# Second-order Hyena filters between the first order's spectral products, and their norms applied after the convolution

## The reference

```
h = sin(fr * (feats @ w1 + b1)); h = sin(fr * (h @ w2 + b2)); h = h @ w3 + b3
h = h.reshape(L, N_DIR, HYENA_ORDER, D_HYENA)            # 512, 2, 2, 512
h = h * exp(-t * abs(decay))
fwd, bwd = h[:, 0], h[:, 1]
k = concatenate([fwd, zero, flip(bwd[1:])])              # circular, length 2L
k = k * rsqrt(sum(k * k, axis=0) + FILTER_EPS)           # one norm per order and channel
k_f = rfft(k)
z = x1 * (irfft(rfft(v) * k_f[:, 0])[:L] + d[0] * v)
z = x2 * (irfft(rfft(z) * k_f[:, 1])[:L] + d[1] * z)
```

## Time and profile before

| | us |
|---|---|
| median of 3 runs (lowest, highest) | 3144.1 (3139.53, 3148.76) |
| time of the profiled execution | 3137.39 |
| its span, first to last instruction | 3135.5 |
| `hyena_spectra`, first product to the next block's first transpose | 951.24 to 1022.29 |
| `hyena_long_convs`, to its last gating | 1022.29 to 1099.6 |

### The profile page before, as it was taken

How to read it: one execution, slowest core, us unless ns; L and a number is a source line. 1 busy time by engine, 2 the same in 40 slices (tenths; PEclk the granted TensorE clock), 3 DMA queues, 4 the chain that set the end, 5 groups by cost and what they waited for, 6 DMA issues and landing times. The chain is left out here.

```text
span 3135.5 us, 40381 instructions
## 1 busy us (share of the span) xinstructions
PE 2786.7 (89%) x17361; PEld 2194.9 (70%) x17361; DVE 1584.6 (51%) x2124; ACT 872.0 (28%) x1114; POOL 388.4 (12%) x368
## 2 busy tenths in 40 slices
PE   7999998778788889999998969589999659899997
PEld 5888875677563777788886844468887445678886
DVE  5555455666665734455544226553354545363342
ACT  3221234111144123322223323332222423332221
POOL 1111000211002001111100001121020100120110
PEclk9999999899889899999998978889999779989998
DMA  5555530000040033455543200223343200223221
GB/s 154 163 165 170 158 105 21 13 3 3 2 129 0 1 108 101 114 167 162 163 158 111 81 19 0 81 68 109 105 149 101 54 30 2 94 72 104 94 94 54
DMA packets 267298, 272.77 MB, mean 87 GB/s; under 512 B 10559, under 2 KB 248102, under 8 KB 266927
## 3 DMA queue, kind: packets, MB, share of 16 engines
q1 hardware_dynamic: 251760, 208.32, 21.7%
q0 software_dynamic: 15360, 61.87, 6.0%
HBM read 268.07 MB, written 2.10 MB: 86 GB/s over the span
## 5 line engine op out<-in xcount | busy, mean ns | idle before, releaser
L863 DVE TENSOR_TENSOR mlp_wl<-mlp_raw,mlp_wh 128x2048 fp32r<-128x2048 f32 x74 | 189.9, 2566 | 277.8 <-ACT mlp_wh L755 277.8
L863 DVE TENSOR_TENSOR mix_wl<-mix_raw,mix_wh 128x2048 fp32r<-128x2048 f32 (+2 forms) x66 | 153.1, 2319 | 236.9 <-ACT mix_wh L755 236.8
L673 PE MATMUL mix_ps<-h_mix_hi,mix_wh 128*128 128x512 f32 x624 | 245.8, 394 | 10.1 <-ACT mix_wh L755 10.1
L675 PE MATMUL mix_ps<-h_mix_lo,mix_wh 128*128 128x512 f32 x624 | 244.3, 391 | 0.0
L755 ACT ACTIVATE mlp_wh<-mlp_raw 128x2048 fp32r<-128x2048 f32 x74 | 140.5, 1899 | 142.7 <-PE mlp_ps L679 88.8
L755 ACT ACTIVATE mix_wh<-mix_raw 128x2048 fp32r<-128x2048 f32 (+2 forms) x66 | 117.6, 1782 | 219.8 <-PE mix_ps L679 162.1
L673 PE MATMUL ffn_ps<-h_rw_hi,ffn_wh 128*128 128x512 f32 x448 | 175.3, 391 | 0.0
L675 PE MATMUL ffn_ps<-h_rw_lo,ffn_wh 128*128 128x512 f32 x448 | 174.3, 389 | 0.0
L679 PE MATMUL mix_ps<-h_mix_hi,mix_wl 128*128 128x512 f32 x624 | 154.2, 389 | 0.0
L673 PE MATMUL mlp_ps<-view,mlp_wh 128*128 128x512 f32 x384 | 150.1, 391 | 0.0
L675 PE MATMUL mlp_ps<-view,mlp_wh 128*128 128x512 f32 x384 | 149.5, 389 | 0.0
(11 more groups left out here) (568 smaller groups left out, 6042.2 us busy)
## 6 DMA issues: line engine op xcount, KB each, us to landing
mlp_raw<-in_mlp_w SPq DMA_DIRECT2D x64, 1024.0 KB, 5.4
ffn_sraw<-in_ada_w POOLq DMA_DIRECT2D x34, 768.0 KB, 5.2
ffn_raw<-in_ffn_w_gu SPq DMA_DIRECT2D x44, 512.0 KB, 5.0
mix_raw<-in_ffn_w_gu SPq DMA_DIRECT2D x44, 512.0 KB, 5.0
mix_sraw<-in_ada_w POOLq DMA_DIRECT2D x22, 768.0 KB, 5.3
mix_raw<-in_a_w_in SPq DMA_DIRECT2D x12, 1024.0 KB, 5.2
mix_sraw<-in_kv_ada_w POOLq DMA_DIRECT2D x12, 768.0 KB, 4.9
ffn_raw<-in_w_in SPq DMA_DIRECT2D x8, 1024.0 KB, 5.3
```

The costliest lines, as they stand in the source:

```text
L673: nc.tensor.matmul(ps[:, it.banks[t], :], w(h, k, t), xh[:, k, :], start=it.first and k == it.k0, stop=False)
L675: nc.tensor.matmul(ps[:, it.banks[t], :], w(h, k, t), xl[:, k, :], start=False, stop=False)
L863: nc.vector.tensor_tensor(slot(wl, it), slot(raw, it), slot(wh, it).bitcast(F32), ALU.subtract)\
```

## The change

The second order's steps are written between the first order's spectral groups, on every engine. `fb` and `sq` get two buffers, `ab` gets its own place for each order (the first order's in free parts of the arena: where the inverse tables and the second order's spectrum will be). The products of step n+1 are written ahead of the sums of step n, the envelopes of n+1 ahead of the squares of n. The sums of squares are no longer spread over all partitions: the squares are the weights, in four 128x128 tiles, and one column of ones is streamed, so that the norm of a channel stands in its own partition (`pn[o]`, 128x4). The root is taken of `rcol` (128x8) at the block's end. The spectra are not scaled; `take_out` of the convolutions multiplies the output by `rcol` in the instruction that adds the bias term, and the bias term itself is made by ACT. The inverse tables (cosT, sinT) are loaded after the first order's spectrum, since their place holds `ab` until then.

```diff
-def hyena_spectra(nc, e, h2, filt, cos, sin, spec):
+def hyena_spectra(nc, e, h2, filt, cos, sin, back_tables, spec, rcol):
...
+        fb = sb("fb", [P, 2, 2, D_HY])
+        sq = sb("sq", [P, 2, 2, D_HY])
+        ab1 = sb("ab", [P, 2, TT, D_HY])
+        ab = ((floats(e, 4, TT), floats(e, 16, TT)), (ab1[:, 0, :, :], ab1[:, 1, :, :]))
-        pn = pb("pn", [P, D_HY])
+        pn = [pb(f"pn{o}", [P, L]) for o in range(2)]
...
+        @block.sync
+        def _(sp):
+            sp.wait_ge(k_done, N)
+            for dst, src in back_tables:
+                sp.dma_start(dst, src).then_inc(back_in, 16)
+            sp.wait_ge(back_in, 16 * len(back_tables))
 
         @block.tensor
         def _(pe):
+            def raw(n):
+                o, t = n // TT, n % TT
+                for d in range(2):
+                    if n > 0:
+                        pe.wait_ge(fb_ready, 2 * (n - 1) + d + 1)
+                    nc.tensor.matmul(ps[:, d, :], h2[:, t * P:(t + 1) * P], w3[:, 2 * d + o, :],
+                                     start=True, stop=True).then_inc(raw_done, 1)
+            def sums(n):
+                o, t = n // TT, n % TT
+                for d in range(2):
+                    pe.wait_ge(sq_ready, 2 * n + d + 1)
+                    for c in range(HT):
+                        last = nc.tensor.matmul(pn[o][:, c:c + 1], sq[:, n % 2, d, c * P:(c + 1) * P], e.ones[:, 0:1],
+                                                start=t + d + c == 0, stop=t == TT - 1 and d == 1 and c == HT - 1)
+                    last.then_inc(sq_used, 1)
+            def spectrum(o, j):
...
-                        nc.tensor.matmul(pn[:, :], e.ones[:, :], sq[:, d, :], start=t == 0 and d == 0,
-                                         stop=t == TT - 1 and d == 1).then_inc(sq_used, 1)
...
+            raw(0)
+            for n in range(TT):
+                raw(n + 1)
+                sums(n)
+            for j in range(4):
+                spectrum(0, j)
+                if j + 1 < TT:
+                    raw(TT + j + 1)
+                sums(TT + j)
+            for j in range(4):
+                spectrum(1, j)
 
         @block.scalar
...
+            envelope(0)
+            for n in range(TT):
+                envelope(n + 1)
+                squares(n)
+            for j in range(4):
+                evens(j)
+                if j + 1 < TT:
+                    envelope(TT + j + 1)
+                squares(TT + j)
+            for j in range(4):
+                evens(4 + j)
+            act.wait_ge(inv_ready, 2)
+            nc.scalar.activation(rcol, rcol, ACT.Sqrt)
 
         @block.vector
...
+            def take_out(o, j):
+                dve.wait_ge(even_out, m + 1)
+                dve.wait_ge(k_done, 2 * m + 2)
...
+            for n in range(TT):
+                step(n)
+            for j in range(4):
+                take_out(0, j)
+                step(TT + j)
+            for o in range(2):
+                inverse(o)
+            for j in range(4):
+                take_out(1, j)
-        @block.gpsimd
...
-                        nc.gpsimd.tensor_tensor(d, d, rs[:, 1, :], ALU.mult).then_inc(scaled, 1)

-def hyena_long_convs(nc, e, uc, z2, cos, sin, cosT, sinT, spec):
+def hyena_long_convs(nc, e, uc, z2, cos, sin, cosT, sinT, spec, rcol):
...
+            def bias(u):
+                o, half = UNITS[u]
+                for c in range(CT):
+                    j, n = CT * half + c, CT * u + c
+                    if u > 0:
+                        act.wait_ge(gated, n - CT + 1)
+                    nc.scalar.activation(dz[:, c, :], source[o][:, j, :], ACT.Copy, scale=col(e, "hy_bias_d", o * HT + j))\
+                        .then_inc(biased, 1)
...
-                    if u > 0:
-                        dve.wait_ge(gated, n - CT + 1)
+                    dve.wait_ge(biased, n + 1)
                     sums = po[:, c, :].rearrange("p (two n) -> p n two", two=2)
...
+                    nc.vector.scalar_tensor_tensor(d, sums, col_at(rcol, o * HT + j), d, ALU.mult, ALU.add)\
                         .then_inc(o_out, 1)
...
-            dense(nc, e, "hy_in", steps, buf(s2, "hy_in"), hyena_filter_mlp(nc, e, I, h2, filt, tables))
+            dense(nc, e, "hy_in", steps, buf(s2, "hy_in"), hyena_filter_mlp(nc, e, I, h2, filt, tables[0:2]))
```

More of the change, by code:

```diff
@@ new lines, in spectrum @@
+            def spectrum(o, j):
+                m = o * 4 + j
+                part, f = j // 2, j % 2
+                if j == 0:
+                    pe.wait_ge(ab_ready, N * (o + 1))
+                if m >= 2:
+                    pe.wait_ge(k_out, 2 * (m - 1))
+                for t in range(TT):
+                    last = nc.tensor.matmul(pk[:, m % 2, t // 2, :], (cos, sin)[part][:, t, f * P:(f + 1) * P],
+                                            ab[o][part][:, t, :], start=t % 2 == 0, stop=t % 2 == 1)
+                    if t % 2 == 1:
+                        last.then_inc(k_done, 1)
@@ new lines, in envelope, with squares @@
+            def envelope(n):
+                o, t = n // TT, n % TT
+                for d in range(2):
+                    if n > 0:
+                        act.wait_ge(fb_ready, 2 * (n - 1) + d + 1)
+                    nc.scalar.activation(env[:, d, :], dec[:, 2 * d + o, :], ACT.Exp,
+                                         scale=negt[:, t:t + 1]).then_inc(env_ready, 1)
+            def squares(n):
+                for d in range(2):
+                    act.wait_ge(fb_ready, 2 * n + d + 1)
+                    if n > 1:
+                        act.wait_ge(sq_used, 2 * (n - 2) + d + 1)
+                    nc.scalar.activation(sq[:, n % 2, d, :], fb[:, n % 2, d, :], ACT.Square).then_inc(sq_ready, 1)
@@ L1342, in _ @@
             st = Steps(steps)
-            for o in range(2):
[L1344 to L1375, removed]
@@ L1377, in _, with step @@
[L1377 to L1389 removed]
+            def step(n):
+                o, t = n // TT, n % TT
+                for d in range(2):
+                    dve.wait_ge(raw_done, 2 * n + d + 1)
+                    dve.wait_ge(env_ready, 2 * n + d + 1)
+                    if n > 1:
+                        dve.wait_ge(sq_ready, 2 * (n - 2) + d + 1)
+                        dve.wait_ge(ab_ready, 2 * (n - 1))
+                    scalar = 1.0 if d == 0 else notfirst[:, t:t + 1]
+                    nc.vector.scalar_tensor_tensor(fb[:, n % 2, d, :], ps[:, d, :], scalar, env[:, d, :],
+                                                   ALU.mult, ALU.mult).then_inc(fb_ready, 1)
+                dve.wait_ge(fb_ready, 2 * n + 2)
+                nc.vector.tensor_tensor(ab[o][0][:, t, :], fb[:, n % 2, 0, :], fb[:, n % 2, 1, :], ALU.add)\
+                    .then_inc(ab_ready, 1)
+                nc.vector.tensor_tensor(ab[o][1][:, t, :], fb[:, n % 2, 0, :], fb[:, n % 2, 1, :], ALU.subtract)\
+                    .then_inc(ab_ready, 1)
@@ L1490, in _ @@
                         .then_inc(even_out, 1)
+                    if f == 1 or u == 0:
+                        continue
+                    bias(u - 1)
+            bias(N - 1)
         @block.vector
```

84 lines of the change are left out of this document (26 added, 58 removed).

## The result

The change makes the kernel slower: the median goes from 3146.4 us (four runs of the kernel before, 3139.5 to 3150.0) to 3174.1 us (four of the kernel after, 3170.6 to 3178.3), +27.6 us. The ratio on record, which is not the quotient of the two medians, is 1.0104 with a 95% interval of 1.0082 to 1.0125, which makes 25.8 to 39.3 us. The forecast was 3171 (3146 to 3184). The profiled execution took 3170.6 us, 33.2 more than that of before: the filter block, from its first product to the first transpose of the convolutions, went from 71.05 us to 1048.96 - 948.38 = 100.58 us (+29.5), and all the rest of the span, whose work is almost the same, from 3064.5 to 3068.2 (+3.7).

A forecast was written before the change was run, and what follows sets the result against it. PE, busy 89% of the span, was taken as the bound. Order 1's spectrum 26.9 us late plus 2.2 at its head gave +29.1, the block's end -2.0: +27.1 on 3144.1, so 3171 us, range 3146 to 3184.

The forecast's parts named there:

- the groups' heads: Start of each spectral group: half clock for some 4.4 us, so a group takes 5.6 us, not 3.43.
- order 0's steps: Filter block's first four steps: at half clock 24.5 us from 954.1, so the first spectrum starts at 978.6.
- the periods: Order 0's groups, each with wait and order 1's step: 13.6 us three times, then 11.1 us.
- the last spectrum's head: First group of order 1's spectrum: starts at half clock and loses 2.2 us.
- The sum records: Sums of squares, 16 single-column records a step: 0.136 us each at full clock, 0.17 at half clock.
- my sign of 0.14 to 0.2: Sign that the forecast is right: 64 sum records an order, 0.14 to 0.2 us apart.
- the 3.7 us of added work: Short sums replacing dense ones at full clock: PE's list longer by 0.47 us a step, over 8 steps.
- My bound of 0.24: Far upper end for a sum record at half clock, in us; would add +9.0 us to the forecast.
- rivals 1 and 2: 1 (0.12): clock full except where it falls today, 3148 us; 2 (0.12): only waits bring it down, 3159 us.
- The waits: Behind order 0's groups: PE stands 2.15 us for DVE's filter, queued behind the take-out; 2.8 us after the fourth.
- The pause: Ahead of the convolutions: shrinks from 4.78 us to about 2.8; -2.0 us as POOL's scalings go.
- Rival 3: Sum records: short products cost less than the side sums show, so not slower, 3137 to 3144 us; chance 0.04.

The follow-up runs named there:

- e4: Kernel after with one swap on DVE, the filter step ahead of the take-out, short sums kept: 3145.5 us against 3140.2 before, ratio 1.0006, block 75.2 us.
- e5: Kernel after with dense sums and DVE's filter step ahead of the take-out: 3138.8 us against 3138.2 before, ratio 0.9996, block 64.8 us.
- e3: Kernel after with the old order of work and dense sums both put back: 3141.1 us against 3140.2 before, ratio 0.9996, block 70.8 us.
- e6: e4 with POOL adding the squares, so PE makes only four short sum products an order: 3126.7 us against 3138.2 before, ratio 0.9960, block 56.3 us.
- e7: Kernel after with filter products filled from 65 to 128 rows with zeros: 3146.2 us against 3138.2 before, ratio 1.0022, block 79.2 us.
- e9: e4 (short sums, filter step first) with filter products filled to 128 rows: 3127.7 us against 3143.0 before, ratio 0.9954, block 60.7 us.
- e1: Kernel after with the old order of work put back, short sums kept: 3156.6 us against 3140.2 before, ratio 1.0037, block 87.1 us.
- e2: Kernel after with dense sums put back, new order kept: 3157.9 us against 3140.2 before, ratio 1.0054, block 83.4 us.
- e8: e6 (POOL adds the squares) with filter products filled to 128 rows: 3126.5 us against 3143.0 before, ratio 0.9940, block 56.2 us.

## Why the prediction was right

The forecast was +27.1 us, the medians differ by 27.6, and the block grew by 29.5. The mechanism was the one named: half clock in the steps, PE standing behind each group for DVE's filter, half clock at the groups' heads. That the medians agree to 0.5 us is luck: the block came out 2.4 us longer than forecast (order 0's steps +3.1, the periods -0.2, the last spectrum's head -0.5), and the interval of the time is 25.8 to 39.3 us. Two terms were off in size.

**The sum records: mis-sized at both clocks, the other way round at each.** They follow each other 0.11 us apart at full clock, where 0.136 was taken from the side sums, and 0.213 at half clock, where 0.17 was taken; my sign of 0.14 to 0.2 missed both. The row of the side sums was misread: their first load, behind a dense product, starts 0.23 us ahead of the second, and the division by five spread that over all; the others start 0.11 us apart. At full clock the short sums of a step cost 1.70 us and the dense ones 1.71: the 3.7 us of added work don't exist. The Trainium skill (TensorE: Matmul & The Clock Gate, LDWEIGHTS (loading the stationary operand)) has a formula in the columns alone, by which a load of 128 takes an estimated 107 ns; my text set that aside on the strength of the misread row. The trace is near it at 2.4 GHz, with 0.11 us, and has about the double at 1.2 GHz, which the page, giving one formula, doesn't tell. My bound of 0.24 held this value; the choice of the middle of the two nearest rows didn't. Only the half-clock value counted here: order 0's spectrum starts 30.5 us into the block where 978.6 - 951.2 = 27.4 was forecast, and 4 x (0.213 - 0.17) x 16 = 2.8 of the 3.1 us are this term.

**Order 0's steps.** Half clock from 950.9 to the first group, with PE busy 28.00 of 28.00 us. This refutes rivals 1 and 2, which both need the full clock there.

**The waits.** 2.15 and 2.8 us were forecast, 2.05 and 2.71 measured, ended by DVE's L1379 and by the squares. The reading of DVE's order is shown by e4 and e5, where the one swap removes all four.

**The periods** (a group of order 0, the wait behind it, and the products and sums before the next group). 13.6 three times and 11.1 was the forecast, 51.9 us; 12.03, 14.88, 12.03 and 12.73 were measured, 51.7 us. The agreement is luck in part: three of the four groups were longer than the 5.6 us taken (up to 6.58), and so were the second and the last run of sums, at half clock (3.41 and 3.57 us), but behind the first and the third wait the products still had the full clock (1.98 us at 986.52 and 1013.62, against 3.38 at 999.35), and the sums behind them had part of it. Order 1's spectrum took 15.65 us, 1.7 more than 13.94; 2.2 was forecast.

**The end and the rest.** The pause shrank by 2.0 us, as forecast. Late tables (3.9 us to landing), bias and root cost nothing that shows: e3 has them, with an inversion in another form, and is at 0.9996; its interval would hide some 5 us. The clock that I left out of the sum behind the shorter pause came back for a moment only: the first eight transposes took 1.19 us, against 1.96, but the clock fell right behind them, and the convolutions took 76.7 us against 77.3.

**Rival 3** had its first half right (0.11 us a record, nil loss) and failed on its condition, the clock.

**Where my account of the clock was incomplete.** The prediction put the half clock down to products of 65 rows and single columns together. e6 shows that back-to-back 65-row products alone keep it at half, e7 and e9 that single-column sums beside 128-row products don't, and e4 that between dense groups neither does. And it undervalued the waits behind the groups: they stood for 8.9 us of standing and, with short sums, for 16.5 us of clock (e4). The two causes overlap: taking the waits away alone gives 25.4 us of block, filling the rows alone 21.4, both together 39.9 (100.6 to 60.7), not 46.8. Part of the loss needs both, so the 29.5 us can't be split between them cleanly.

**What stays open.** The rest of the span, almost the same code, came out between 3063.7 and 3076.9 us in eleven profiles, and the block's start between 948.4 and 953.9 in the seven kernels with identical code ahead of it (the kernel after and e1 to e6). Block lengths come from one profile each and may scatter too, so that differences of a few us between them are not firm. Why e5's 6 us of block don't show in its time is not settled; e9's 10 us of block lie within its interval.

## What to carry to other kernels

A product that streams one column isn't free: here 16 such records took 1.70 us at full clock, as long as the four dense ones that they replaced. What the replacement took away was the dense work that kept the clock up, and a cheap way to have the clock back was to fill a product of 65 rows up to 128 with zeros. When work is put between an engine's groups to fill it, look at the engine that feeds it: the feeding step belongs ahead of the taking out in that engine's program, and here this one swap was worth 25 us of block (18.5 with the dense sums, e2 against e5). Read PEclk in the same stretch as the busy time, since a PE that is 100% busy may be so because it is slow.

## What the runs showed of the hardware that was not expected

- Back-to-back fp32 records with a 128x128 weight load and one streamed column start 0.11 us apart at a granted clock of 1.00 and 0.213 at 0.50; the load as recorded goes from 0.19 to 0.33 us.
- The number of rows that a product uses can decide at which clock it runs. With 65 rows PE was at 0.50 for 28.00 us of unbroken work; with 128 rows, the rest alike, at 1.00 (e7, e9) behind the early spell.
- Pauses of 2.05 us were followed by half clock in the products or the group behind them in the kernel after; without the pauses the same stretch had 0.93 (e4). The Trainium skill (TensorE: Matmul & The Clock Gate, Why this matters for your kernels) warns of longer idle gaps only; the trace disagrees, with these 2.05 us.
- The convolutions took 76.7 us at a mean clock of 0.91 (kernel after) and 70.6 at 1.00 (e3) with the same code. A saving of a few us in one block can drown in that.
- A DVE sum of two SBUF tiles of 128x512 went from 0.69 to as much as 1.80 us while POOL added tiles of the same size (e8).
